# A transformer layer on one core: the first expert tile leaves PSUM ahead of the low parts of the next weight chunk

## What is computed

```python
hu = lax.ragged_dot(xs, w_gate_up, group_sizes) + b_gate_up[e_sorted]   # xs: rows x 1024, w: 1024 x 2048 per expert
gate = jnp.minimum(hu[:, :D_FF], 7.0)
up = jnp.clip(hu[:, D_FF:], -7.0, 7.0)
act = (up + 1.0) * gate * jax.nn.sigmoid(1.702 * gate)
y = lax.ragged_dot(act, w_down, group_sizes) + b_down[e_sorted]
```

## Time and profile before

| | |
|---|---|
| median of three runs | 4730.74 us |
| the profiled execution, its own time | 4728.68 us |
| its span, first to last instruction | 4726.8 us |
| TensorE matmul, busy | 4364.9 us (92%) |
| VectorE, busy | 3097.0 us (66%) |
| ScalarE, busy | 1819.1 us (38%) |
| mean granted TensorE clock | 0.956 |
| experts' first matmul | at 2003.8 us |

### The profile page before, as it was taken

How to read it: one execution, slowest core, us unless ns; L and a number is a source line. 1 busy time by engine, 2 the same in 40 slices (tenths; PEclk the granted TensorE clock), 3 DMA queues, 4 the chain that set the end, 5 groups by cost and what they waited for, 6 DMA issues and landing times. The chain is left out here.

```text
span 4726.8 us, 69036 instructions
## 1 busy us (share of the span) xinstructions
PE 4364.9 (92%) x24163; PEld 3174.3 (67%) x24163; DVE 3097.0 (66%) x4884; ACT 1819.1 (38%) x2677; POOL 930.0 (20%) x1126
## 2 busy tenths in 40 slices
PE   8999978889988887399999999999999999999987
PEld 4444434444444444299989989888898898998961
DVE  2567747886778884345556656666576776776757
ACT  1222233343433333133334444444444545554530
POOL 0000012121211112211212212222122222222235
PEclk9999989999999898699999999999999999999986
DMA  5344221010010001344446446464656566566578
GB/s 186 118 121 122 65 92 30 15 29 15 20 23 15 15 13 18 95 162 151 151 144 221 169 163 219 156 226 171 217 180 234 193 240 230 188 248 217 188 241 337
DMA packets 525083, 666.35 MB, mean 141 GB/s; under 512 B 59200, under 2 KB 389440, under 8 KB 524896
## 3 DMA queue, kind: packets, MB, share of 16 engines
q1 hardware_dynamic: 400368, 484.87, 30.5%
q10 hardware_dynamic: 97984, 93.93, 6.0%
q0 software_dynamic: 26576, 85.56, 4.6%
HBM read 543.93 MB, written 120.36 MB: 141 GB/s over the span
## 5 line engine op out<-in xcount | busy, mean ns | idle before, releaser
L1952 DVE TENSOR_TENSOR w_lo<-w_raw,w_hi 128x2048 fp32r<-128x2048 f32 x386 | 874.6, 2287 | 570.2 <-ACT w_hi L2036 570.2
L1863 PE MATMUL gu<-x_hi,w_hi 128*128 128x240 f32 (+8 forms) x4096 | 1200.4, 293 | 33.1 <-DVE up L1967 27.6
L1864 PE MATMUL gu<-x_lo,w_hi 128*128 128x240 f32 (+8 forms) x4096 | 1196.0, 292 | 0.0
L1865 PE MATMUL gu<-x_hi,w_lo 128*128 128x240 f32 (+8 forms) x4096 | 1195.2, 292 | 0.0
L2036 ACT ACTIVATE w_hi<-w_raw 128x2048 fp32r<-128x2048 f32 x386 | 726.6, 1907 | 263.8 <-issue 144.9
L1863 PEld LDWEIGHTS gu<-x_hi,w_hi 128*128 128x128 f32 x4096 | 775.7, 189 | 37.7 <-DVE up L1967 31.5
L1864 PEld LDWEIGHTS gu<-x_lo,w_hi 128*128 128x128 f32 x4096 | 776.2, 190 | 0.2
L1865 PEld LDWEIGHTS gu<-x_hi,w_lo 128*128 128x128 f32 x4096 | 776.0, 189 | 0.0
L1837 POOL TENSOR_TENSOR a_lo<-up,a_hi 128x384 fp32r<-128x384 f32 x256 | 396.9, 1550 | 1186.0 <-ACT a_hi L2048 1186.0
L533 PE MATMUL proj_acc<-w_in_sb,hT 128*128 128x512 f32 (+1 forms) x1280 | 495.9, 535 | 0.7 <-ACT hT L549 0.7
L1863 PE MATMUL yp<-w_hi,a_hi 128*128 128x512 f32 x1088 | 445.4, 409 | 2.3
(11 more groups left out here) (299 smaller groups left out, 5736.4 us busy)
## 6 DMA issues: line engine op xcount, KB each, us to landing
w_raw<-w_gate_up SPq DMA_DIRECT2D x258, 1024.0 KB, 7.9
w_raw<-w_down SPq DMA_DIRECT2D x128, 1024.0 KB, 6.9
y_dram<-y_rows ACTq DMA_DIRECT2D x128, 256.0 KB, 4.3
y_dram<-zeros ACTq DMA_DIRECT2D x12, 2688.0 KB, 14.4
h_blk<-h_dram SPq DMA_DIRECT2D x32, 512.0 KB, 6.8
y_dram<-y_rows ACTq DMA_DIRECT2D x128, 128.0 KB, 6.0
qi_dram<-qi_stage ACTq DMA_DIRECT2D x16, 640.0 KB, 3.2
x_in<-x SPq DMA_DIRECT2D x16, 512.0 KB, 6.4
```

What stands on the lines that cost most here:

```text
L1863: nc.tensor.matmul(out, s_hi_, m_hi, start=(n == 0), stop=False)
L1864: nc.tensor.matmul(out, s_hi_, m_lo, start=False, stop=False)
L1865: op = nc.tensor.matmul(out, s_lo_, m_hi, start=False, stop=(n == len(pairs) - 1))
L1952: nc.vector.tensor_tensor(w_lo[:, c % 2, cols], raw[:, c % 3, cols], w_hi[:, c % 2, cols].bitcast(F32), ALU.subtract).then_inc(s_lo, 1)
```

## The change

In the loop over c, the first round (c = 0) takes tile 0 out of PSUM first, and makes both low parts of chunk 1 behind it. The other rounds are as before.

```diff
                     for c in range(4):
                         if c:
                             out_of_psum(v, 2 * c - 1, e)
-                        low(v, c + 1, 0)
-                        if c:
+                            low(v, c + 1, 0)
                             activate(v, 2 * c - 1)
-                        low(v, c + 1, 1)
-                        out_of_psum(v, 2 * c, e)
+                            low(v, c + 1, 1)
+                            out_of_psum(v, 2 * c, e)
+                        else:
+                            out_of_psum(v, 0, e)
+                            low(v, 1, 0)
+                            low(v, 1, 1)
                         activate(v, 2 * c)
```

## The result

The changed kernel takes 4739.31 us (median of 20 runs) where the kernel before, on the same chip, takes 4730.62 us (20 runs): a ratio of 1.0018, 95% interval [1.0012, 1.0025], 8.7 us more. The prediction said 4724.4 us, with a range from 4719 to 4736.

What follows compares the result with a forecast made beforehand. TensorE's stall before tile 2, waiting for VectorE to hand back tile 0's PSUM buffer, was taken as the bound in narrow visits. Stalls +1.7 and clock -8.0 gave -6.3 us: 4724.4 us from 4730.7, range 4719 to 4736.

Steps and rivals of the forecast that it cites:

- the first of the sum: VectorE's gate of tile 0: starts 0.35 us after the tile's last load ends when it waits for TensorE alone.
- the 7.12 us from tile 0's last load to tile 2: TensorE's start of tile 2: 0.35 to gate, 2.16 to low part, 4.49 for the pair, 0.12 to TensorE.
- Stalls at 240: TensorE's wait before tile 2, twelve visits of width 240: 26.4 us shrinks to 20.2, -6.2 us.
- The clock: Granted clock behind tile 2's stall in narrow visits: five falls of 1.6 us each vanish, -8.0 us.
- Widths 272, 288, 304: Tile 2 stalls grow as the low parts come later: +5.0, +1.5 and +1.4 us.
- Width 256: Tile 2 stall in three visits: 4.1 us as before, change 0.
- Stalls alone: All tile 2 stalls over the widths, without the clock: +1.7 us.
- Sum: Whole kernel: stalls +1.7 and clock -8.0 give -6.3 us, median 4724.4 us.
- The rivals: Four other outcomes: falls stay (0.12), more falls (0.06), no losses at 272 to 304 (0.10), nothing happens (0.04).
- The clock falls stay: Rival: falls behind tile 2 hang on the stall's place, not length; only stalls count, +1.7, 4732.4 us; chance 0.12.
- The other side, slower: Slower by more than 9.5 us, chance 0.07; mainly the rival of seven more clock falls, +12.9, 4743.6 us, chance 0.06.

Runs made afterwards that it cites:

- the record: First measurement pair with traces: kernel before 4730.62 us, changed kernel 4739.31 us, ratio 1.0018.
- d3: Changed kernel, chunk 1's high parts issued between the last store's copy and its two DMAs: 4718.36 us (0.9988); again on another chip 4735.6 us (1.0024).
- d2: Changed kernel, all three row gathers behind tile 0, row list still loaded at the head: 4719.86 us (0.9991); again on another chip 4721.86 us (0.999).
- the last group: One chip: changed kernel again 4739.99 us; third gather behind tile 0, 4718.28 us; kernel before with early high parts, 4690.72 us.
- h2: Changed kernel, only the third row gather moved behind tile 0, the first two at the head: 4718.28 us, ratio 0.9983 to the kernel before.
- e3: Changed kernel, ScalarE making chunk 1's high parts ahead of the previous visit's last down-tile copy and store: 4726.01 us, ratio 0.9997 to the kernel before.
- group 1: One chip: whole gather moved in changed kernel 4741.85 us, in kernel before 4742.2; tile 0 split 4708.85; kernel before with early high parts 4695.7.
- e4: Changed kernel, only tile 0's gate and up half ahead of the low parts, clip and product behind: 4708.85 us (0.9953); again 4702.61 us (0.9951).
- group 3: One chip: changed kernel again 4714.07 us (0.9982); row gathers behind tile 0, 4719.86 us; high parts ahead of the store DMAs, 4718.36 us.
- e5: Kernel before, ScalarE making chunk 1's high parts ahead of the previous visit's last down-tile copy and store: 4695.7 us (0.9927); again 4690.72 us (0.9924).

## Why the prediction was wrong

- **The step that failed** is the first of the sum: "A gate that waits for TensorE alone starts 0.35 us after its tile's last load ends". I took it from tile 5 of a visit and applied it to tile 0. For tile 0 it is 0.33 us where the release is on time, and 0.96 us in the late one shown, so there the 7.12 us from tile 0's last load to tile 2 are short by 0.61. In the trace of before no gate of tile 0 in a narrow visit waited for TensorE, so its row couldn't show it; only the semaphore's own record did, and I didn't read it.
- **Stalls at 240**, -6.2 us: -6.4 where releases are on time (20.0 against 26.4), +0.2 in the record.
- **The clock**, -8.0 us: no falls in the changed kernel where its releases are on time; five in the record, as before. The 1.68 us stall keeps the clock and the 2.05 to 2.5 us one often doesn't, so this term hung on the first. In the seven traces of the kernel before, the changed one and d3 with late releases the falls come behind stalls of 1.90 to 2.59 us, 35 in all, and no stall of up to 1.78 us had one.
- **Widths 272, 288, 304**, +5.0, +1.5 and +1.4 us: measured in the record +6.0, +1.5 and +1.5. The single stalls on time are 1.05, 0.75 and 0.37 us, against 1.04, 0.75 and 0.36; two of the six at 272 were late as well. This part was right to 0.02 us. **Width 256**, 0: right on time (4.08 us), +1.5 when late.
- **Stalls alone**, +1.7 us: +1.9 on time, +10.8 in the record. The 9 us between are the late releases.
- **Sum**, -6.3 us: on the chip without late releases 4714.07 against 4723.66, -9.6 us, with an interval from -13 to -4. The mechanism and its sizes were right there, as far as one side shows it: no trace of the kernel before was taken on that chip, so the falls that it saves there weren't seen. Elsewhere it was +8.7, +11.9, +9.0 and +13.6 us.
- **The rivals.** "The clock falls stay" was right in half of it, for a reason that it didn't name: they stayed because the stalls did. The other side, slower, came by a way that none of the rivals had.

**What makes the release late.** In nine traces 146 releases are late, and 142 of them come 1.57 to 2.03 us after the start of the third gather's record, that is 0.6 to 1.1 us after its end; the other four come 0.91 to 0.99 us after the start. In wide visits tile 0 ends after that moment and is on time, which is why lateness grows toward the narrow visits and why it never met a later tile. Shown is that it needs the third gather at the head (d2 and the last group). The Trainium skill, "Perfetto Trace Analysis", section "DMA Instruction — SWDGE (GPSIMD)", says that such a record ends when the descriptors are written, not when the data has moved; the trace agrees, since the data lands 7.4 us after issue. The packet records place the data: the same 142 releases come within 0.4 us of the first packet that GpSimd's queue moves for the gathers of that visit. It is data of the first gather and not of the third: where the third stands apart (h2), its packets start 4.2 us or more after it. But in h2 the queue starts as early in the visit as in the control, and no release is late. So it is something that comes with the third gather's issue, and not the start of the transfers, that holds the release back; which part of the issue stays open.

The third gather isn't enough, though: in e3 twelve releases of tile 0 fell due 1.0 to 1.3 us after its start and came on time. Nor are the stores of the last down tile needed, as e3's two late releases show. **Open** stays why two chips don't do it: group 1 has no late release in kernels with gathers and stores in place (e4), and group 3 has none in any. One thing goes with it that no run separates. The traces of the four groups with late releases lack 390 to 1056 of some 18,400 records of DMA completions, those of groups 1 and 3 at most 23. The recording may bring the delay, or both may be signs of a third thing; every time here comes with a recorded span, so no run tells.

## What to carry to other kernels

A wait that was covered before is not known to be short: before an edit uncovers it, read when its own semaphore rises, at that very place in the loop and not at a similar one. Here the exposed instruction sat next to a gather, and the shorter path lost what it had gained; the order that keeps the cover and makes the high parts earlier instead (e5) won 0.75% on both chips that it ran on. And a gain of 0.2% measured on one chip can have the other sign on the next, so a claim of that size needs more than one chip, or a mechanism that is seen in the trace.

## What the runs showed of the hardware

- A semaphore that a matmul raises came 0.4 to 1.1 us after that matmul's start, in two cases 1.5 and 1.6, instead of 0.3, when it fell due within about 1.6 us of the start of the third of three gathers by GpSimd; in four of the six groups of runs, and in the other two never.
- Stalls of some 2 us let the granted clock fall to 1.2 GHz for about 3 us, but not each: of the stalls of 1.85 us and more in those seven traces, 35 had a fall and 48 had none, and the longest without one was 2.84 us. The Trainium skill, "TensorE: Matmul & The Clock Gate", section "Why this matters for your kernels", warns of longer gaps only; the runs show that these are enough.
- Two visits with the same width and the same stall can differ by 0.4 us: at 272 with 1.05 us of stall they take 81.98 or 82.37 us, one value or the other, for the tiles behind the stall are issued at one of two paces (125.3 or 126.7 ns from load to load). What picks the pace wasn't tried.
- ScalarE's DMAs aren't held by the activation in front of them (rows of d3): to delay such a DMA, what feeds it has to come later.
